# A two-layer hybrid decoder trunk on one core: ScalarE's planned order made to count table loads, and x1 transposed from scaled rows

## The chip, the core and the metric

One core of one Trainium2 chip runs one launch of the kernel. The metric is device time in microseconds (us), the median of the runs of that kernel. Engines are written as in the profile: PE (TensorE; its weight loads are PEld), ACT (ScalarE), DVE (VectorE), POOL (GpSimd), SP (SyncE).

## What is computed

The reference is a trunk of `DEPTH = 2` layers over 512 tokens of width 1024, all in float32. Cut to what matters here:

```python
def hybrid_layer(x, ...):
    h = rms_norm(x, ln_mix_pre)
    # one projection h @ w_in, split into the inputs of three mixers and the gate logits
    y_a = dsa_attention(qa, ka, a_v, iq, ik, i_w)        # A: per query the top 128 keys, softmax over them
    o_b = gated_delta_rule(qb, kb, vb, g, beta)          # B: chunked scan with a triangular inverse
    y_b = rms_norm(o_b, gdn_norm) * silu(b_z)
    o_c = retention(qc, kc, vc)                          # C
    y_c = rms_norm(o_c) * silu(c_g)
    merged = sum(sigmoid(gate_i) * (y_i @ w_branch_i))
    x = x + rms_norm(merged @ w_out, ln_mix_post)        # "x1" below
    ff = square(relu(rms_norm(x, ln_mlp_pre) @ w_up)) @ w_down
    return x + rms_norm(ff, ln_mlp_post)                 # "x2" below
```

## The kernel before

Every large product is made of float32 data split into two parts, hi and lo: `passes` (L1068 to L1071) issues three matmuls for one product, hi by hi, lo by hi and hi by lo. Weights come in slabs of 128 x 1024 (512 KB). For each slab SP issues the load, POOL rounds it to the hi part (`w_hi`, L1046 and L1047), DVE subtracts to get the lo part (`w_lo`, L979, a step called `lo`), and PE uses both. There are two slots, so slab n + 2 is loaded and rounded only after PE is done with slab n. A layer has 136 slabs: 76 in the mixing half, the rest in the MLP.

The mixing half is laid out by a planner, `schedule()`, in plain Python before the kernel is built. It holds a list of steps for PE, ACT and DVE with a cost, their predecessors and a rank (the length of work behind a step). It repeatedly takes the step that can start first; among steps of one engine that could start at the same moment it takes the highest rank. Its result is a fixed order per engine (`PE_ORDER`, `ACT_ORDER`, `DVE_ORDER`), which each engine then follows strictly. Dense products are cut in four pieces (`piece`), so that small products can stand between them. A tail that is written out by hand (the `tail` list: gates and merge of branch B, and `stay` steps) follows the planned part. In it, `every` puts each `lo` step behind the DVE step of a slab.

Steps that the change and the prediction touch:

- ACT's `fin` (L1721 to L1728). It finishes branch C and later branch B, four heads each: `fin_sq` squares (L1719), PE sums over partitions (L1361), `fin` takes Ln (L1726) and Exp (L1728), and DVE multiplies (L2143, L2145). A function that is not in the table set loaded last costs an ACT_TABLE_LOAD, which the build places before it. The code loads the set that has both Ln and Exp before head 0 alone (L1723). The gate steps `cg`, `z`, `gate` and `mgate` use Tanh (L1752, L1758, L1771), for which the other set is loaded. When a Tanh has stood between two heads, Ln and Exp each get a load of their own.
- In the order of before, ACT does, for branch C: `fin 0, gate 2, fin 1, fin_sq 2, fin 2, fin_sq 3, gate 3, fin 3`. The planner counts no table loads.
- The end of the mixing half, on DVE: `merge B 2` first makes four `a_lo` parts (`lo_merged`, L2182), waits for PE's merge slab, and combines (L2197, L2203). Then comes the `lo` step of slab 75, the first slab of the output projection, then `merge B 3` with two more `a_lo` parts.
- The output projection: one slab (k = 0 and 1) for all four token tiles into psM, then the seven "staying" slabs, per token tile t (`out_tile`, L1415). `TURNS` says before which of these seven PE turns a finished x1 tile: `(2, 2): 0` is "while working on token tile 2, before its slab 2, turn x1 tile 0".
- A finished token tile t: ACT squares, DVE multiplies with the gain (L2232), adds (L2248), ACT squares again, DVE makes a 128 x 128 diagonal matrix of the row scales (`diagonal`, L804), PE multiplies x1 by it eight times (`turn_x1`, L1428), which transposes and scales at once. ACT and DVE take hi and lo parts from PSUM (L1807, L2238). The first two MLP slabs are done for tiles 0 to 2 first (`up_tokens`), then tile 3 is turned, then tile 3 is done for both.
- The end: per token tile, DVE makes x2 over 1024 columns (L2344), and SP writes it out (L2354).

## Time and profile before

| | us |
|---|---|
| three runs | 1933.62, 1933.68, 1937.95 |
| median | 1933.68 |
| the profiled execution, as timed | 1936.01 |
| its span in the profile | 1934.2 |
| PE busy in it | 1895.0 (98%) |
| ACT busy, with 29 table loads of 1.28 | 497.0 (26%) |
| DVE busy | 1131.6 (59%) |

The profile lists, for each engine, what it did and what it waited for; a wait is put down to the instruction that came last. "PEclk" in a view of stretches is the granted clock of TensorE: 1.00 is 2.4 GHz, 0.50 is 1.2 GHz. The two layers run the same code one after the other; layer 0 ends and layer 1 begins near 970 us, and the same instruction of layer 1 comes some 957 us after that of layer 0 in the mixing half.

### The profile page before, as it was taken

The page shows a single profiled execution, that of the slowest core. Times are in us where ns is not written, and L with a number is a line of the kernel's source. Part 1 is how long each engine was busy: PE and PEld are TensorE (multiplying, and loading weights), DVE is VectorE, ACT ScalarE, POOL GpSimd, SP SyncE. Part 2 cuts the span into 40 slices and gives each one's busy share as a digit, 9 for nine tenths or more (in the row PEclk, how much of TensorE's full clock was granted, in tenths as well). Part 3 has the DMA queues.
Part 4 walks back from the last instruction along what each step waited for, and adds up shares of the span by engine and source line. Part 5 has one row for each costly group of instructions (what it writes and reads, how often), then busy time and mean ns, then how long its engine had stood idle before and what let it go on. Part 6 is the DMA issues. An engine that isn't in the chain of part 4 may idle for free.

```text
span 1934.2 us, 25057 instructions
## 1 busy us (share of the span) xinstructions
PE 1895.0 (98%) x8862; PEld 1534.1 (79%) x8862; DVE 1131.6 (59%) x1910; ACT 497.0 (26%) x971; POOL 353.9 (18%) x549
## 2 busy tenths in 40 slices
PE   8999999999999999999999999999999999999998
PEld 6877767788788888888878767677888888888886
DVE  6865778843465642454477658887535655425534
ACT  3163352312334100011222533534132331000101
POOL 2221111111220222222112211111102102222220
PEclk9999999999999999999999999999999989999999
DMA  6432222322520422223223322222215222222221
GB/s 240 142 120 82 68 69 80 93 66 66 195 99 20 145 94 94 96 98 98 77 95 102 126 66 77 66 80 87 80 53 217 66 77 97 93 95 96 98 98 55
DMA packets 72478, 186.79 MB, mean 97 GB/s; under 512 B 18304, under 2 KB 30784, under 8 KB 71488
## 3 DMA queue, kind: packets, MB, share of 16 engines
q1 hardware_dynamic: 41328, 152.10, 23.3%
q10 hardware_dynamic: 31056, 33.38, 5.1%
q8 instruction: 66, 1.08, 0.2%
q14 instruction: 28, 0.23, 0.0%
HBM read 174.40 MB, written 11.06 MB: 96 GB/s over the span
## 4 chain that ended last, share of the span: by engine, by line
PE 92%; ACT 4%; DVE 3%; issue 1%; DMA 0%; POOL 0%; SPq 0%; DVEq 0%; ACTq 0%; POOLq 0%
PE psD L1069 23%; PE psD L1071 23%; PE psD L1070 23%; PE psM L1069 4%; PE psM L1070 4%; PE psM L1071 4%; PE psM L1128 2%; PE psM L1142 1%; PE psM L1337 1%; PE psM L1234 1%; PE psM L1135 1%; PE psM L1355 1%; PE psM L1343 1%; PE psM L1361 1%; PE psM L1226 1%
## 5 line engine op out<-in xcount | busy, mean ns | idle before, releaser
L1069 PE MATMUL psD<-a_hi,w_hi 128*128 128x512 f32 (+2 forms) x1488 | 597.7, 402 | 2.4 <-DVE a_lo L2238 1.5
L1071 PE MATMUL psD<-a_hi,w_lo 128*128 128x512 f32 (+2 forms) x1488 | 577.8, 388 | 0.0
L1070 PE MATMUL psD<-a_lo,w_hi 128*128 128x512 f32 (+2 forms) x1488 | 576.8, 388 | 0.0
L979 DVE TENSOR_TENSOR w_lo<-raw,w_hi 128x1024 fp32r<-128x1024 f32 x208 | 254.2, 1222 | 295.9 <-POOL w_hi L1047 294.9
L1046 POOL TENSOR_TENSOR w_hi<-raw,tabs 128x1 fp32r<-128x1 f32 x272 | 65.6, 241 | 1541.7 <-PE psD L1071 1324.0
L1069 PEld LDWEIGHTS psD<-a_hi,w_hi 128*128 128x128 f32 (+1 forms) x1488 | 281.2, 189 | 74.7 <-issue 18.0
L1070 PEld LDWEIGHTS psD<-a_lo,w_hi 128*128 128x128 f32 (+1 forms) x1488 | 281.3, 189 | 58.6 <-issue 4.8
L1071 PEld LDWEIGHTS psD<-a_hi,w_lo 128*128 128x128 f32 (+1 forms) x1488 | 280.9, 189 | 58.4
L1047 POOL TENSOR_SCALAR w_hi<-raw 128x1023 fp32r<-128x1023 f32 x272 | 296.9, 1092 | 0.0
L1836 ACT CAST f_hi<-gt 128x512 f32 x64 | 39.9, 623 | 480.2 <-DVE gt L2270 480.2
L2267 DVE TENSOR_SCALAR gt<-psD 128x512 f32<-128x512 f32 x64 | 44.3, 691 | 140.0 <-PE psD L1071 140.0
L1069 PE MATMUL psM<-w_hi,f_hi 128*128 128x512 f32 x256 | 99.6, 389 | 0.0
L1070 PE MATMUL psM<-w_lo,f_hi 128*128 128x512 f32 x256 | 99.6, 389 | 0.0
L1071 PE MATMUL psM<-w_hi,f_lo 128*128 128x512 f32 x256 | 99.6, 389 | 0.0
L1069 PE MATMUL psD<-y_hi,w_hi 128*128 128x512 f32 x192 | 77.5, 404 | 1.7 <-issue 1.7
L2259 DVE TENSOR_TENSOR w_lo<-raw,w_hi 128x1024 fp32r<-128x1024 f32 x64 | 78.2, 1222 | 1.4 <-POOL w_hi L1047 1.4
L1071 PE MATMUL psD<-y_hi,w_lo 128*128 128x512 f32 x192 | 74.9, 390 | 0.0
L1070 PE MATMUL psD<-y_lo,w_hi 128*128 128x512 f32 x192 | 74.7, 389 | 0.0
L1069 PE MATMUL psD<-w_hi,f_hi 128*128 128x512 f32 x192 | 74.7, 389 | 0.0
L1070 PE MATMUL psD<-w_lo,f_hi 128*128 128x512 f32 x192 | 74.7, 389 | 0.0
L1071 PE MATMUL psD<-w_hi,f_lo 128*128 128x512 f32 x192 | 74.7, 389 | 0.0
L1574 ACT COPY wide<-psD 32x512 f32<-32x512 f32 (+1 forms) x84 | 48.7, 580 | 72.8 <-DVE cqk L1944 21.0
(272 smaller groups left out, 2580.1 us busy)
## 6 DMA issues: line engine op xcount, KB each, us to landing
raw<-in_ws SPq DMA_DIRECT2D x272, 512.0 KB, 3.2
s_raw<-in_wo ACTq DMA_DIRECT2D x14, 512.0 KB, 11.9
out<-x SPq DMA_DIRECT2D x8, 512.0 KB, 5.6
x<-rows_d ACTq DMA_DIRECT2D x4, 1024.0 KB, 5.7
x<-out ACTq DMA_DIRECT2D x2, 2048.0 KB, 8.5
e_raw<-in_wo ACTq DMA_DIRECT2D x8, 512.0 KB, 7.4
tabs<-in_tab SPq DMA_DIRECT2D x1, 2944.0 KB, 12.0
x<-in_x SPq DMA_DIRECT2D x4, 512.0 KB, 5.2
```

The source lines that it names most:

```text
L979: dve.tensor_tensor(w_lo[:, s, :], raw[:, s, :], w_hi[:, s, :].bitcast(F32), ALU.subtract) \
L1046: pool.tensor_tensor(w_hi[:, s, 0:1], raw[:, s, 0:1], T("ones")[:, 0:1], ALU.mult)
L1047: pool.tensor_scalar(w_hi[:, s, 1:], raw[:, s, 1:], 1.0, 1.0, ALU.mult, ALU.mult) \
L1069: pe.matmul(out, lhi, rhi, start=start, stop=False)
L1070: pe.matmul(out, lhi, rlo, start=False, stop=False)
L1071: return pe.matmul(out, llo, rhi, start=False, stop=stop)
L1128: ins = pe.matmul(ps[:, cut(h)], lhs(h), rhs(h), start=True, stop=True)
L1135: ins = pe.matmul(ps[:, h * P // 2:(h + 1) * P // 2], lhs[:, cut(h)], blocks(rhs[:, cut(h)], l, odd), start=True, stop=True)
L1574: sig(act.copy(wt[to:to + n, 6 + r % 2, :], src[at:at + n, :]), "rot_copy" if to + n == P else "rot_part")
L1836: act.copy(f_hi[:, bass.ds(it * 4 + i, 1), :].rearrange("p a s -> p (a s)"), gt[:, i, :]).then_inc(*inc("f_hi", 1, FG // 4))
L2259: dve.tensor_tensor(w_lo[:, s, :], raw[:, s, :], w_hi[:, s, :].bitcast(F32), ALU.subtract) \
L2267: dve.tensor_scalar(gt[:, i, :], psD[i][:, :], 0.0, None, ALU.max) \
```

## The change

Five edits in one:

1. The planner has a table `TABLES` of which steps need which table set. An ACT step that needs another set than the last one is planned 1.28 us longer, and when several ACT steps could start at the same moment, such a step counts with a rank lower by 2.56. The build loads the Ln and Exp set before any `fin` that follows a step of the other set, not before head 0 alone.
2. For x1 tiles 0 to 2, DVE writes scaled rows (two operations of 128 x 512) in place of the diagonal matrix, and PE transposes them against the identity. Tile 3 stays as it was. Tile 2 is turned one slab later.
3. The `a_lo` parts of the merged tiles are DVE steps of their own (`low`), and the `lo` step of slab 75 moves ahead of `merge B 2`.
4. The seven "staying" loads signal on two semaphores (three loads, four loads) in place of seven.
5. In the last layer, x2 is made and written out in halves of 512 columns.

```diff
-TURNS = {(2, 2): 0, (2, 5): 1, (3, 5): 2}
+TURNS = {(2, 2): 0, (2, 5): 1, (3, 6): 2}
...
+TABLES = {"silu": "exp", "cg": "exp", "z": "exp", "gate": "exp", "mgate": "exp", "decays": "log", "fin": "log"}
...
+    def loads(n):
+        return 1.28 if n[0] == "act" and TABLES.get(n[1], tables) != tables else 0.0
...
-            n = max((n for n in names if starts[n] <= first + 1e-9), key=lambda n: rank[n])
+            n = max((n for n in names if starts[n] <= first + 1e-9), key=lambda n: rank[n] - 2 * loads(n))
...
+        t += loads(n)
+        tables = TABLES.get(n[1], tables) if e == "act" else tables
...
+    final = max(s for s in closed if s[1] == "lo")
+    closed.remove(final)
+    for lows, j in (((0, 1, 2, 3), 2), ((4, 5), 3)):
+        i = closed.index(("dve", "merge", "B", j))
+        closed[i:i] = [("dve", "low", k) for k in lows] + ([final] if j == 2 else [])
...
+            def scaled(norm, t):
+
+                r = rstd(norm, t, 1)
+                for half in range(2):
+                    w = slice(half * S, (half + 1) * S)
+                    sig(dve.tensor_scalar(wide[:, t, w], x[:, t, w], r, None, ALU.mult), "rows_" + norm)
...
-                                ins = pe.matmul(x1_T(t, k), x[:, t, cut(k)], wide[:, t, 0:P], start=True, stop=True)
+                                if t < READY:
+                                    ins = pe.transpose(x1_T(t, k), wide[:, t, cut(k)], T("ident"))
+                                else:
+                                    ins = pe.matmul(x1_T(t, k), x[:, t, cut(k)], wide[:, t, 0:P], start=True, stop=True)
...
                     def fin(br, h):
-                        if h == 0:
-                            act.preload_act_table_set("natural_log_exp_and_others")
...
                     def stay(j):
-                        act.wait_ge(*on(f"stay_in{j}", 16))
+                        if j == 0:
+                            act.wait_ge(*on("first_in", 16 * 3))
+                        if j == 3:
+                            act.wait_ge(*on("stay_in", 16 * (len(STAYING) - 3)))
...
+                    tables = "exp"
                     for kind, *args in ACT_ORDER:
+                        if TABLES.get(kind, tables) != tables:
+                            tables = TABLES[kind]
+                            if kind == "fin":
+                                act.preload_act_table_set("natural_log_exp_and_others")
...
-                        diagonal("pre_mlp", t)
+                        if t < READY:
+                            scaled("pre_mlp", t)
+                        else:
+                            diagonal("pre_mlp", t)
...
-                        sig(dve.scalar_tensor_tensor(out=x[:, t, :], in0=wide[:, t, :], scalar=r,
-                                                     in1=x[:, t, :], op0=ALU.mult, op1=ALU.add), "x2")
+                        for w in (slice(0, D),) if layer < DEPTH - 1 else (slice(0, S), slice(S, D)):
+                            sig(dve.scalar_tensor_tensor(out=x[:, t, w], in0=wide[:, t, w], scalar=r,
+                                                         in1=x[:, t, w], op0=ALU.mult, op1=ALU.add), "x2")
```

## Rows read from the trace of the kernel before

**Rows 1.** The page's part 1: busy us, share of the span, instructions.
```profile
PE 1895.0 (98%) x8862; PEld 1534.1 (79%) x8862; DVE 1131.6 (59%) x1910; ACT 497.0 (26%) x971; POOL 353.9 (18%) x549
```

**Rows 2.** Waits of PE over the span: us in total, times, longest.
```profile
PE psM L1361 <- ACT sqs L1719: 5.7, 3, 2.6
PE psM L1069 <- DVE w_lo L979: 2.2, 2, 1.1
PE psM L1142 <- ACT x L1670: 2.2, 2, 1.1
...
PE psM L1343 <- DVE small L2129: 2.0, 2, 1.0
```

**Rows 3.** Groups by line of ACT: table loads in the two lines of `fin`.
```profile
L1726 ACT ACT_TABLE_LOAD x6 | 7.7, 1283 | 0.1
L1728 ACT ACT_TABLE_LOAD x6 | 7.7, 1283 | 0.1
```

**Rows 4.** Stretches: length, PE, PEld, DVE, ACT, POOL busy, PEclk, DMA.
```profile
279.00:281.00 2.00, 2.00 (x7) 1.51 (x6) 1.39 (x4) 1.99 (x3) 0.00 (x0) 0.50 0.00 0
```

**Rows 5.** Stretches, start of layer 1's MLP.
```profile
1584.00:1588.00 4.00, 4.00 (x18) 3.90 (x18) 2.18 (x3) 0.62 (x1) 0.55 (x2) 0.50 0.83 316
```

**Rows 6.** Timeline of DVE (start us, us): MLP ReLU steps 1 and 3, layers 0 and 1.
```profile
624.92 0.69 DVE L2267 TENSOR_SCALAR gt<-psD 128x512 f32<-128x512 f32 x1 [1.18 <-PE psD L1071]
...
633.37 0.69 DVE L2267 TENSOR_SCALAR gt<-psD 128x512 f32<-128x512 f32 x1 [0.90 <-PE psD L1071]
...
1582.28 0.69 DVE L2267 TENSOR_SCALAR gt<-psD 128x512 f32<-128x512 f32 x1 [1.24 <-PE psD L1071]
...
1595.29 0.69 DVE L2267 TENSOR_SCALAR gt<-psD 128x512 f32<-128x512 f32 x1 [4.73 <-PE psD L1071]
```

**Rows 7.** Stretches, the end of the top-k work in layer 0.
```profile
350.00:369.00 19.00, 19.00 (x98) 16.02 (x97) 16.95 (x31) 3.47 (x7) 4.48 (x6) 1.00 0.44 145
```

**Rows 8.** Timeline of PE around the turn of x1 tile 0.
```profile
588.94 0.39 PE L1071 MATMUL psM<-s_hi,a_lo 128*128 128x512 f32 x1
589.16 1.95 PE L1428 MATMUL psM<-wide,x 128*128 128x128 f32 x16
590.87 0.48 PE L1069 MATMUL psM<-s_hi,a_hi 128*128 128x512 f32 x1
```

**Rows 9.** Timeline of PE around eight transposes of attention weights.
```profile
253.48 0.40 PE L1071 MATMUL psD<-a_hi,w_lo 128*128 128x512 f32 x1
253.72 1.03 PE L1142 MATMUL psM<-tabs,pr 128*128 128x128 f32 x8
254.50 0.48 PE L1069 MATMUL psD<-a_hi,w_hi 128*128 128x512 f32 x1
```

**Rows 10.** Groups of DVE by form: a row scale from SBUF over 512 columns.
```profile
L2098 DVE TENSOR_SCALAR sc<-rl,small 128x512 f32<-128x512 f32 x2 | 1.0, 480 | 0.0
```

**Rows 11.** Timeline: DVE's diagonals of x1 tiles 2 and 3, PE's turn of tile 3.
```profile
605.99 0.29 DVE L804 TENSOR_SCALAR wide<-tabs,small 128x128 f32<-128x128 f32 x1
...
617.40 0.29 DVE L804 TENSOR_SCALAR wide<-tabs,small 128x128 f32<-128x128 f32 x1
...
619.32 1.95 PE L1428 MATMUL psM<-wide,x 128*128 128x128 f32 x16
```

**Rows 12.** Timeline at the end of the mixing half: slab 75's rounding, then `merge B 2`.
```profile
556.02 1.51 POOL L1047 TENSOR_SCALAR w_hi<-raw 128x1023 fp32r<-128x1023 f32 x1
...
557.99 1.27 DVE L2197 SCALAR_TENSOR_TENSOR mt<-gt,psD 128x512 f32<-128x512 f32 x2
```

**Rows 13.** Timeline of DVE: the last x2 tile.
```profile
1929.91 1.28 DVE L2344 SCALAR_TENSOR_TENSOR x<-wide,small,x 128x1024 f32<-128x1024 f32 x1
```

**Rows 14.** Stretches at the end of the span.
```profile
1932.50:1933.00 0.50, 0.00 (x0) 0.00 (x0) 0.00 (x0) 0.00 (x0) 0.00 (x0) 0.50 0.99 401
```

**Rows 15.** Timeline of DVE: one round of the top-k search over 512 keys.
```profile
368.76 0.68 DVE L2115 MATCH_REPLACE8 work<-small,work 128x512 f32<-128x512 f32 x1
...
369.47 0.69 DVE L2113 MAX8 small<-work 128x8 f32<-128x512 f32 x1
```

More of the change, by code:

```diff
@@ L388, in schedule @@
     free = {"pe": 0.0, "act": 4.0, "dve": 5.0}
-    end, out = {}, []
+    end, out, tables = {}, [], "log"
+    def loads(n):
+        return 1.28 if n[0] == "act" and TABLES.get(n[1], tables) != tables else 0.0
     dense, halved, acc = [("act", "cv", 3)] * ST, None, None
@@ L804, in diagonal @@
                 sig(dve.tensor_scalar(wide[:, t, 0:P], T("ident"), r, None, ALU.mult), "diag_" + norm)
-            return total, rstd, diagonal
+            def scaled(norm, t):
[3 more added lines that the diff above has]
+                    sig(dve.tensor_scalar(wide[:, t, w], x[:, t, w], r, None, ALU.mult), "rows_" + norm)
+            return total, rstd, diagonal, scaled
         def signals(eng, who):
@@ L1035, in _ @@
                 seen, sig, own = signals(dve, "dve")
-                total, rstd, diagonal = dve_norm(dve, sig, own)
+                total, rstd, diagonal, scaled = dve_norm(dve, sig, own)
                 dve.wait_ge(kept["basics_in"], 16)
@@ L1420, in turn_x1 @@
                     def turn_x1(t):
-                        pe.wait_ge(*on("diag_pre_mlp", t + 1))
                         for i in range(2):
+                            if t < READY:
+                                pe.wait_ge(*on("rows_pre_mlp", 2 * t + i + 1))
+                            else:
+                                pe.wait_ge(*on("diag_pre_mlp", 1))
                             if t == 2:
@@ L1866, in _ @@
                     seen, sig, own = signals(dve, "dve")
-                    total, rstd, diagonal = dve_norm(dve, sig, own)
+                    total, rstd, diagonal, scaled = dve_norm(dve, sig, own)
                     def f32(ap):
@@ L2186, in merge @@
                         b = "AB".index(br)
-                        if b and j >= 2:
-                            for k in (range(4), range(4, 6))[j - 2]:
-                                lo_merged(k)
                         slab(dve, ("merge", br, j))
@@ L2210, in _ @@
                              "split": split_y,
-                             "mergeC": mergeC, "merge": merge, "stay": stay}
+                             "mergeC": mergeC, "merge": merge, "stay": stay, "low": lo_merged}
                     for kind, *args in DVE_ORDER:
@@ L2249, in _ @@
                                                      in1=x[:, t, :], op0=ALU.mult, op1=ALU.add), "x1")
-                        diagonal("pre_mlp", t)
+                        if t < READY:
+                            scaled("pre_mlp", t)
+                        else:
+                            diagonal("pre_mlp", t)
                         for i in {1: (0, 1), 2: (2,)}.get(t, ()):
@@ L2352, in _ @@
                         for t in range(ST):
-                            sp.wait_ge(*on("x2", t + 1))
-                            sp.dma_start(out[:, t * D:(t + 1) * D], x[:, t, :]).then_inc(kept["x_saved"], 16)
-                        sp.wait_ge(kept["x_saved"], 16 * ST * (DEPTH + 1))
+                            for half in range(2):
+                                sp.wait_ge(*on("x2", 2 * t + half + 1))
+                                sp.dma_start(out[:, t * D + half * S:t * D + (half + 1) * S], x[:, t, half * S:(half + 1) * S]) \
+                                    .then_inc(kept["x_saved"], 16)
+                        sp.wait_ge(kept["x_saved"], 16 * ST * (DEPTH + 2))
                 before.update(counted - before)
```

2 lines of the change are left out of this document (1 added, 1 removed).

## The prediction

> **What bounds the kernel now.** I read the page's first part, then the waits of PE, then the stretches around each of those waits, and last the timelines. PE is busy for 1895.0 of 1934.2 us [rows 1], so a change can only pay in three ways: less work on PE, fewer waits of PE, or a shorter head or tail. Outside head and tail the waits are few and all lie in the mixing half and at the x1 tiles. The largest is PE waiting for ACT's squares in `fin`, 5.7 us in three places: 2.6 in each layer and 0.5 in layer 1 [rows 2]. PE waits 1.1 us per layer for the lo part of slab 75, and about 1.0 us each for two steps of the last attention block, per layer [rows 2]. ACT (26%) and DVE (59%) are far from full over the span, but not everywhere: from 350 to 369 us DVE is busy 16.95 of 19.00 us [rows 7]. That stretch is the top-k search, which runs in DVE's fixed order, and work of PE that depends on it can't be moved earlier by a faster PE.
>
> **Table loads.** The groups of ACT show six loads at the Ln and six at the Exp of `fin`, 1283 ns each, with 0.1 us of idle time ahead of them all together [rows 3]. They are the heads 1, 2 and 3 of branch C in two layers. With the load at head 0 and the one at the next gate, branch C has 8 loads per layer, 8 x 1.28 = 10.3 us of ACT in about 20 us. `fin_sq 2` stands behind four of them in ACT's order, and PE waits for it. In the new order I follow the planner's rule. Planned 1.28 us longer, `fin 0` ends late enough that `fin 1` is ready beside `gate 2` and has the higher rank, so the two heads go together under one load. `fin_sq 2` is next by rank, then `gate 2`, `fin_sq 3`, and `fin 2` and `fin 3` together, then `gate 3`. That is four loads in place of eight, and `fin_sq 2` moves ahead of `gate 2`, about 3 x 1.28 = 3.8 us earlier, more than the wait of 2.6. So I take the 5.7 us of wait as gone. What is late next is `gate 2`, some 3 us later; its PSUM bank is wanted again only four dense tiles later, some 20 us. Branch B's four heads stand together already, so nothing changes there. The penalty on the rank acts only when two steps tie, so the planned 1.28 us is what moves things. It moves them from the first `cg` step on, in all three orders, for the rest of the mixing half. I can't cost that from rows; I take zero with both signs kept open in the rivals.
>
> There is a second cost of this wait in the profiled execution. Behind it the granted clock is 0.50 (1.2 GHz), for example from 279 to 281 us [rows 4]; that stretch at half clock costs some 3.4 x 0.5 = 1.7 us. It does not follow the same wait in layer 1. A longer one lies at the start of layer 1's MLP [rows 5]: there the ReLU steps of layer 1 lag those of layer 0 by 1582.28 - 624.92 = 957.36 us before and by 1595.29 - 633.37 = 961.92 us behind it, 4.56 us more [rows 6]. The three timed runs spread over 4.3 us, about one such fall. I leave one of the longer kind in the median of before and after alike.
>
> **x1 as scaled rows.** A turn by the diagonal is 8 matmuls that show as 16 records, and from the last dense matmul before it to the first one behind it 590.87 - 588.94 = 1.93 us pass, less one ordinary step of 0.23: 1.70 us of PE [rows 8]. Eight transposes show as 8 records and take 254.50 - 253.48 = 1.02 less 0.23 = 0.79 us [rows 9]. So each of the three turns saves 0.91 us, 6 x 0.91 = 5.5 us in both layers, all on PE. DVE pays for it: two operations of 128 x 512 with a row scale. The nearest row for one is 0.48 us [rows 10], so 0.96 in place of 0.29. They would be 1.4 if they ran like an ordinary two-operand step (0.69 for each half); I take 0.96, from the row of the same operation. For tile 2 the diagonal was done at 606.28 [rows 11], directly ahead of the turn. Now PE arrives there 2 x 0.91 = 1.8 us earlier, ACT and DVE get tile 2 earlier by the same, and the turn is one slab (6 x 0.23 = 1.4 us) later, which covers the extra 0.67. Behind it only one slab (1.4 us) in place of two (2.7) covers the making of tile 2's hi and lo parts before `up_tokens` wants them, and they can begin only 0.45 earlier after the turn's start, a half turn being that much shorter: little or no slack is left. Tile 3 is similar: its diagonal is done at 617.69 and PE turned it at 619.32 [rows 11], 1.6 us of slack. PE now comes 2.7 us earlier, the chain of tile 3 only 1.2, as ACT's and DVE's hi and lo work on tile 2 stands in its way. Slack about 0.1. I charge 0.25 us per layer for these two near ties.
>
> A rule of the Trainium skill speaks against this edit. In these rows the dense matmul behind the eight transposes starts without a longer step, at the full clock [rows 9]. "TensorE: Matmul & The Clock Gate", Part 4, says of PE's transposes that they do not count as busy time for the monitor that grants the clock. By that rule less counted work at the turns could bring on the fall of the clock that layer 1 shows at its MLP, and the sum would be less favourable by one such fall or two.
>
> **The lo step of slab 75.** Its hi part is rounded by 556.02 + 1.51 = 557.53, and DVE turns to `merge B 2` at 557.99 [rows 12]. So in its new place ahead of `merge B 2` the step doesn't wait for POOL, runs ahead of the four operations of `merge B 2` in place of behind them, and PE's wait goes: 2.2 us in both layers [rows 2], and 0.1 each of a slower first matmul, 2.4. Behind it in DVE's queue stands `merge B 2`, 1.2 us later, and with it two hi parts of ACT. `merge B 3` had waited for the same lo step and those hi parts, so it starts where it did; if it didn't, PE has 24 matmuls of slab 75 (5.5 us) to run before it wants the banks of `merge B 3`. Making the `a_lo` parts steps of their own changes nothing in order. The two semaphores in place of seven: all seven loads have landed when the first `stay` runs (there is no wait of ACT for them), so zero; if they were late, the first copy would wait for two more loads of 1.3 us each.
>
> **Output in halves.** The last x2 runs from 1929.91 for 1.28 us [rows 13]; SP then writes 512 KB, and the transfer runs at up to 401 GB/s [rows 14], so 1.3 us. With halves the second half is written from about 1931.35 (0.15 later) with 0.65 us of transfer left: 0.65 - 0.15 = 0.5, less a second issue, so 0.4. It can't cost more than a second fixed issue, 0.2 us.
>
> **The sum.** 5.7 (waits of `fin`) + 5.5 + 2.4 + 0.4 = 14.0, less 2 x 0.25 = 13.5 us. Part of the 5.7 I expect back as longer waits in the last attention block, where DVE is nearly full [rows 7]: DVE, too, waited in the `fin` block, so most of it moves along; I charge 0.25 per layer. That makes 13.0: 1933.7 - 13.0 = 1920.7 us. Against the profiled execution's own time the half clock behind `fin` goes as well: 1936.0 - 13.0 - 1.7 = 1921.3. That execution lies 2.3 us above the median, and the two agree within 0.6.
>
> **The rivals.**
> - The `fin` part pays nothing (0.22), in one of two ways. Either PE gets to the last attention block earlier and waits there for DVE's top-k in its place; for it speaks the full DVE [rows 7], against it that DVE's own waits in the `fin` block go too. Or the change doesn't do what it says: the planner, whose penalty acts only on ties, still alternates `fin` and gates, the loads stay near eight per layer, and the wait stays. 1920.7 + 5.2 = 1925.9. The count of loads tells the two apart.
> - The new order is better than mine (0.12): with table loads counted, half of the other waits of the attention part, about 2.5 us per layer, goes too. 1920.7 - 5.0 = 1915.7.
> - The clock falls once more, or twice (0.08), at the x1 turns and MLP starts, by the mechanism shown in layer 1 at 4.56 us each [rows 6]: 1920.7 + 4.6 = 1925.3 to 1929.8. The page named above would have this one. For it speaks that the fall in layer 1 came some us after the x1 turns; against it, that layer 0 has the same work and no fall.
> - Slower (0.05): the replanned order puts rounds of the top-k search for the last block behind other work of DVE, and PE, out of dense pieces by then, waits for them. A planner's step of the search is two rounds, 2 x (0.68 + 0.69) = 2.7 us and more [rows 15]. Four such steps late, in two layers, cost 8 x 2.8 = 22.4: 1943.1. It decides from 13.0 + 5.8 = 18.8 us, or 9.4 per layer, between three and four steps late. Against it: in the planner's own reckoning DVE's work doesn't grow, and the rank of these steps is set by hand and unchanged.
>
> **How the numbers follow.** The forecast has 0.53, with its own range from 1917.5 to 1924: the near ties and the unknown replan at 1.5 us per layer each way. The range for 8 in 10 takes in most of the rivals at 1915.7 and 1925.9 and the first fall of the clock: 1914.5 to 1928. A measurement of this kernel can tell 0.3%, 5.8 us, from no change, so faster means below 1927.9: 0.53 + 0.12 + nearly all of 0.22, which has 2 us of margin, and half of 0.08, which makes 0.87; I take 0.85 as falls of the clock differ between runs. Same: 0.10. Slower: 0.05.
>
> **What would show it.** Right: table loads fall from 29 to about 21, none at an Exp; L1361 is gone from PE's waits; `turn_x1` for tiles 0 to 2 shows 48 records where it showed 96, with 0.8 us each on PE; no wait of PE at the first output slab; the last transfer ends some 0.4 us earlier behind PE's end. Wrong: L1361 still waits, or the waits at L1343 and L1142 grow by what it lost; PE waits for x1's rows (L1428's line) or for `a_lo` in `up_tokens` by more than 0.5 us; stretches at PEclk 0.50 behind the turns in both layers. The prediction as a whole fails if the replanned middle of the mixing half, about 170 us per layer, holds waits that before doesn't have.

## The result and the profile after

The changed kernel takes 1921.22 us in the median of 5 runs (1914.49 to 1925.78). The kernel before takes 1933.62 us beside it (5 runs, 1933.08 to 1937.95). The ratio is 0.9926, with a 95% interval of 0.9911 to 0.9942. The forecast was 1920.7 us, faster. The profiled execution of after is the one at 1925.78 us, with a span of 1924.0 us. One run of one experiment, the x1 rows alone, took 2180.43 us at a mean clock of 0.82, a slow execution, and is left out of its times below.

The runs of after spread over 11 us, and they line up with the mean granted clock that each run lists: 1914.49 at 0.999, 1916.91 at 0.998, 1921.22 at 0.996, 1921.44 at 0.995 and 1925.78 at 0.993. So differences of a few us are compared below at equal clock where I can. For the kernel before, the 66 runs beside the experiments give 1931.5 us on average at 0.998 (3 runs), 1933.5 at 0.997 (17), 1934.4 at 0.996 (19), 1935.9 at 0.995 (13), 1937.8 at 0.994 (8) and 1940.8 at 0.993 (5); one run at 0.991 took 1942.5. The clock is listed in steps of 0.001, each about 1.9 us here, so a comparison at equal clock is good to 1 or 2 us, no closer. Where a stretch of the traces holds the whole effect, it is the better measure.

Part 1 of the page of after (busy us, share of the span, instructions) answers [rows 1]:

```profile
PE 1893.1 (98%) x8814; PEld 1533.2 (80%) x8814; DVE 1133.0 (59%) x1920; ACT 486.9 (25%) x963; POOL 352.9 (18%) x549
```

PE has 48 fewer records, ACT has lost 10.1 us. That is eight table loads at 1.28 us, so 21 are left of 29. The waits of PE in after (us in total, times, longest) answer [rows 2]:

```profile
PE psM L1163 <- ACT x L1697: 2.2, 2, 1.1
PE psM L1364 <- DVE small L2162: 2.0, 2, 1.0
...
PE psD L1090 <- DVE a_lo L2267: 1.5, 2, 0.7
```

The two largest removable waits are gone: PE's wait for ACT's squares (`fin`, now L1382) and its wait for the lo part of slab 75. The waits of the attention part are what they were, and no wait has come in their place. Heads 2 and 3 of `fin` in branch C look like this on ACT, layer 0 (start us, us; [rows 3] are its loads before):

```profile
272.99 1.28 ACT L1783 ACT_TABLE_LOAD   x1
...
278.34 1.28 ACT L1814 ACT_TABLE_LOAD   x1
279.63 0.60 ACT L1751 ACTIVATE sqs<-psM 128x512 f32<-128x512 f32 x1
280.26 0.63 ACT L1753 ACTIVATE sqs<-sqs 128x512 f32<-128x512 f32 x1
280.80 0.58 ACT L1751 ACTIVATE sqs<-psM 128x512 f32<-128x512 f32 x1
281.41 0.63 ACT L1753 ACTIVATE sqs<-sqs 128x512 f32<-128x512 f32 x1
282.06 1.28 ACT L1783 ACT_TABLE_LOAD   x1
```

The two heads stand together between one load at L1814 (Ln and Exp) and one at L1783 (Tanh). On PE the sums of heads 2 and 3 now follow each other in one interruption of the dense stream, 4 matmuls together:

```profile
277.00 0.60 PE L1163 MATMUL psM<-tabs,qkv 128*128 128x128 f32 x4
277.44 1.06 PE L1149 MATMUL psM<-qkv 128*128 128x128 f32 x8
278.33 1.88 PE L1382 MATMUL psM<-sqs,tabs 128*128 128x512 f32 x4
279.65 0.79 PE L1090 MATMUL psD<-a_hi,w_hi 128*128 128x512 f32 x1
```

The turn of x1 tile 0, which [rows 8] show before, and the rows of tile 2 on DVE:

```profile
583.72 0.39 PE L1092 MATMUL psM<-s_hi,a_lo 128*128 128x512 f32 x1
583.95 1.03 PE L1453 MATMUL psM<-tabs,wide 128*128 128x128 f32 x8
584.74 0.47 PE L1090 MATMUL psM<-s_hi,a_hi 128*128 128x512 f32 x1
...
599.03 0.88 DVE L825 TENSOR_SCALAR wide<-x,small 128x512 f32<-128x512 f32 x2
```

From the last dense matmul to the next one 1.02 us pass, less the ordinary 0.23: 0.79 us. The list of PE's waits has none for a row. The end of the mixing half, where [rows 12] are those of before:

```profile
552.18 1.51 POOL L1068 TENSOR_SCALAR w_hi<-raw 128x1023 fp32r<-128x1023 f32 x1
554.16 1.21 DVE L1000 TENSOR_TENSOR w_lo<-raw,w_hi 128x1024 fp32r<-128x1024 f32 x1
555.29 1.27 DVE L2226 SCALAR_TENSOR_TENSOR mt<-gt,psD 128x512 f32<-128x512 f32 x2
```

The lo step of slab 75 now stands ahead of `merge B 2`, 0.47 us behind POOL's rounding. Last, the granted clock. In after it falls to 0.50 for some 10 us at the start of the MLP of both layers; before has this only in layer 1 [rows 5]. A shorter fall, of some 3.4 us, lies at 1333 us in after. Stretches (length, PE, PEld, DVE, ACT, POOL busy, PEclk, DMA share, GB/s):

```profile
616.00:620.00 4.00, 4.00 (x24) 4.00 (x23) 2.53 (x3) 0.01 (x1) 1.21 (x2) 0.56 0.67 180
620.00:624.00 4.00, 4.00 (x16) 3.71 (x16) 2.15 (x5) 0.60 (x1) 1.21 (x2) 0.50 0.93 328
...
1576.00:1580.00 4.00, 4.00 (x14) 3.48 (x14) 2.33 (x3) 0.62 (x1) 1.21 (x2) 0.50 1.02 415
```

### The profile page after: what moved, and what is told of

Its sections match the earlier page's. It is cut to its first block, busy times and chain, and to the rows that moved or that the text cites. A ratio compares the mean times of both kernels' runs of the same rounds, so it can differ in the third digit from the quotient of the medians.

```text
span 1924.0 us, 24975 instructions
## 1 busy us (share of the span) xinstructions
PE 1893.1 (98%) x8814; PEld 1533.2 (80%) x8814; DVE 1133.0 (59%) x1920; ACT 486.9 (25%) x963; POOL 352.9 (18%) x549
## 4 chain that ended last, share of the span: by engine, by line
PE 94%; ACT 3%; DVE 2%; issue 1%; DMA 0%; DVEq 0%; SPq 0%; ACTq 0%
PE psD L1090 24%; PE psD L1092 24%; PE psD L1091 24%; PE psM L1092 4%; PE psM L1091 4%; PE psM L1090 4%; PE psM L1149 2%; PE psM L1163 1%; PE psM L1358 1%; PE psM L1255 1%; PE psM L1156 1%; PE psM L1376 1%; PE psM L1364 1%; PE psM L1382 1%; PE psM L1247 1%
```

## The experiments

The first theory is that of the prediction: four separate gains, of which `fin` and the x1 rows carry nearly all. The rivals are that the clock, not the waits, makes a good part of the difference, and that some gains cover or undo each other. I took each part alone on top of before, took one part out of after, and then worked on the two points left over, tile 3's wait and the clock. "Alone" always leaves the rest of before as it is.

### The pair again

Before against itself, and after a second time beside other runs.

> The kernel before, unchanged, to have the granted clock of each of its runs. Theory of the sum: the scatter of 4 to 5 us between runs of one kernel is the number of falls of the clock (some 4.4 us each for a long one, 1.7 for a short one), so a run with fewer falls is faster by that. Run without any: about 1929; most runs at 1933 to 1934 with a mean clock of 0.996 to 0.997; a run at 1938 has a lower mean clock, 0.993 to 0.995. Rival: the scatter is not the clock; runs at 1933 and at 1938 then show the same mean clock.

> The changed kernel, unchanged, for more of its runs with their clocks. Theory of the sum plus falls: without falls (mean clock 0.999) 1914.5 to 1915.5, against 1929.8 for before extrapolated to that clock; each 0.001 of mean clock less costs some 1.5 to 2 us; median 1918 to 1922. If the clock falls as in before, the median is 15 us below before; if rows of x1 bring falls of their own, the median is only 11 to 13 us below, and runs at mean clock 0.996 or less are more than half.

Before again: 1935.14 us, ratio 0.9998 (0.9985 to 1.001); its profile has the waits of [rows 2], only that L1361 has 5.2 us in two places in place of 5.7 in three. The clock is at 0.50 behind the wait of `fin`, this time in both layers (from 278 to 280 us in layer 0). The fall and the missing third wait go together, as is shown below.

After again: 1915.89 us (1913.57 to 1924.62, 6 runs), ratio 0.9912 (0.9892 to 0.9931). That is 5.3 us under the first series of the same kernel. Two of these 6 runs have a mean clock of 0.996 or less, against three of the first 5. Its profile has the clock at full speed where after's first one has it at half:

```profile
616.00:620.00 4.00, 3.98 (x29) 3.58 (x29) 3.00 (x4) 0.62 (x1) 2.37 (x4) 1.00 0.77 226
620.00:624.00 4.00, 4.00 (x19) 3.33 (x18) 3.31 (x5) 0.62 (x1) 0.00 (x0) 1.00 1.01 402
```

At equal clock the two kernels stand apart by 15.0 us at 0.998 (1931.5 against 1916.5, the mean of 1916.91 and 1916.18), 13.3 at 0.996 (1934.4 against 1921.1), 14.4 at 0.995 (one run of after) and 15.6 at 0.993.

### Each part alone

The planner counts loads, the loads are made as needed, and the order follows; nothing else.

```diff
+TABLES = {"silu": "exp", "cg": "exp", ..., "decays": "log", "fin": "log"}
+    def loads(n):
+        return 1.28 if n[0] == "act" and TABLES.get(n[1], tables) != tables else 0.0
-            n = max(..., key=lambda n: rank[n])
+            n = max(..., key=lambda n: rank[n] - 2 * loads(n))
+        t += loads(n)
```

> Edit 1 alone: the planner counts table loads, and the Ln and Exp set is loaded before any fin that follows the other set. Theory of the sum: table loads 21, PE's wait at the fin line gone (5.7 us), no other wait grown by more than 0.5 per layer: 5.2 us less than before at equal clock, so about 1928.5 if the clock falls as often. Rival (given back): the wait appears again at the last attention block (the smax and turn lines), and the time is within 1.5 us of before.

1924.38 us (1922.73 to 1934.41, 7 runs), ratio 0.9947 (0.9929 to 0.9966): 10.4 us under the 1934.8 us of before, twice what was forecast. At equal clock it is 7.0 us (1924.55 against 1931.5 at 0.998) and 6.3 at 0.993 (one run). The wait for the squares is gone, the others are unchanged, and the load order is that of after. Part of it can be read straight off the loads. The stretch from the load at the first gate of branch C to the one at `fin` of branch B is that of these rows, first before again, then this kernel:

```profile
222.07 1.28 ACT L1752 ACT_TABLE_LOAD   x1
...
487.70 1.28 ACT L1723 ACT_TABLE_LOAD   x1
```

```profile
221.91 1.28 ACT L1759 ACT_TABLE_LOAD   x1
...
482.73 1.28 ACT L1793 ACT_TABLE_LOAD   x1
```

265.63 us have become 260.82. In layer 1 it is 265.84 and 261.20. In the profile of before the clock doesn't fall there in layer 1, and the stretch is 264.92 us, so the `fin` part is worth 3.7 to 4.1 us in that layer with no fall of the clock in it. The other traces say the same. Five profiled executions have the order of before, so ten such stretches: 264.46 and 264.92 us without a fall, 265.39 to 265.84 with one fall behind the wait of `fin`, and 266.91 to 267.40 with one there and another some 105 us later. The new order gives 260.49 to 261.50 in 15 stretches without a fall, 260.9 on average; against 264.7, the mean of the two, that is 3.8 us. One fall behind `fin` costs 0.5 to 1.4 us. The rest of the difference of the medians, some 3 us, I put down to the clock, as 6 of 7 runs have a mean clock of 0.998 or 0.999, where most runs of before have 0.995 to 0.997; no trace of those other runs exists.

What the 3.7 to 4.1 us consist of can be read from PE's gaps in layer 1, where neither trace has a fall. First before, then this kernel, with the same small matmuls in the gaps:

```profile
1231.58 0.39 PE L1071 MATMUL psD<-a_hi,w_lo 128*128 128x512 f32 x1
1234.59 1.12 PE L1361 MATMUL psM<-sqs,tabs 128*128 128x512 f32 x2 [2.62 <-ACT sqs L1719]
1235.16 0.79 PE L1069 MATMUL psD<-a_hi,w_hi 128*128 128x512 f32 x1
...
1238.10 0.39 PE L1071 MATMUL psD<-a_hi,w_lo 128*128 128x512 f32 x1
1238.97 1.12 PE L1361 MATMUL psM<-sqs,tabs 128*128 128x512 f32 x2 [0.48 <-ACT sqs L1719]
...
1241.18 0.47 PE L1069 MATMUL psD<-a_hi,w_hi 128*128 128x512 f32 x1
```

```profile
1229.36 0.39 PE L1080 MATMUL psD<-a_hi,w_lo 128*128 128x512 f32 x1
...
1232.24 0.79 PE L1078 MATMUL psD<-a_hi,w_hi 128*128 128x512 f32 x1
```

Before has gaps of 3.58 and 3.08 us from one dense matmul to the next, less 0.23 each: 6.20. The new order has one of 2.88, so 2.65. That makes 3.55 us. The listed waits are 2.62 + 0.48 = 3.10 of it. Another 0.32 comes from how a wait is listed, namely from the end of the record before it: dense matmuls start every 0.23 us, but each record is 0.39 long, so each of these two waits costs 0.16 us more than is listed. For the sums standing in one group only 0.13 is left.

The second wait, of 0.48 us, is there just in the stretches in which the clock doesn't fall behind the first (layer 1 of before, layer 0 of the halves alone, at 281.38 us). With the fall, PE reaches the sums of head 3 later and finds them ready. That is part of why a fall there costs less than the 1.7 us that it takes from PE.

The x1 rows alone. Seven semaphores become two here too, to free some for the new signals of the rows; that edit has no run of its own.

```diff
+                                if t < READY:
+                                    ins = pe.transpose(x1_T(t, k), wide[:, t, cut(k)], T("ident"))
-                        diagonal("pre_mlp", t)
+                        if t < READY:
+                            scaled("pre_mlp", t)
```

> Edit 2 alone, with edit 4 (two semaphores for the staying loads in place of seven, which only frees semaphores). Theory of the sum: each of six turns takes 0.80 in place of 1.70 to 1.77 us on PE, 5.5 in all, less small new waits: the first MLP ReLU step comes 2.6 to 2.8 us earlier behind the end of the mixing half in each layer; about 1928.5 at equal clock. Rival (skill's rule on transposes): the clock falls after the turns in both layers in most runs, mean clock lower than before by 0.002 or more, and the time is 1929 to 1933.

1928.89 us (1928.13 to 1929.77, 6 runs), ratio 0.9963 (0.995 to 0.9976), 5.9 us less. At 0.996 it is 1928.8 against 1934.4, 5.6 less, at 0.995 6.1 less, but at 0.998 (2 runs) only 2.8 less. The trace is clearer. From the last dense matmul ahead of the turn of tile 0 to the first ReLU step of the MLP, 35.98 us pass in before ([rows 8] and [rows 6]); here it is 33.36, in both layers:

```profile
590.80 0.39 PE L1078 MATMUL psM<-s_hi,a_lo 128*128 128x512 f32 x1
...
624.16 0.69 DVE L2286 TENSOR_SCALAR gt<-psD 128x512 f32<-128x512 f32 x1 [1.18 <-PE psD L1078]
```

The eight profiled executions with diagonals have 35.97 to 36.05 there, after again has 33.29 and 33.31. So the rows give 2.6 to 2.7 us per layer, 5.3 in all, on top of before as in after. The wait for the squares stands as it did (5.2 us), so this part adds to the `fin` part. No wait of PE for rows is listed. The recorded rival isn't seen: the mean clock of these runs is 0.995 to 0.998, that of before beside them 0.991 to 0.998, and no MLP in this profile has a fall.

The low steps alone.

```diff
+    final = max(s for s in closed if s[1] == "lo")
+    closed.remove(final)
+    for lows, j in (((0, 1, 2, 3), 2), ((4, 5), 3)):
+        i = closed.index(("dve", "merge", "B", j))
+        closed[i:i] = [("dve", "low", k) for k in lows] + ([final] if j == 2 else [])
```

> Edit 3 alone: the a_lo parts as steps, the lo step of slab 75 ahead of merge B 2. Theory of the sum: PE's wait before the first output slab (1.1 us per layer) goes and nothing comes in its place: 2.4 us less, 1931.2 at equal clock. Rival: merge B 3 becomes later, PE waits for its banks at the first staying slab by about 1 us per layer, and the time is that of before within 0.5 us.

1931.87 us (1929.52 to 1934.22, 12 runs), ratio 0.9978 (0.9967 to 0.9989), 2.9 us less; at 0.997 it is 1931.5 against 1933.5, 2.0 less, and at 0.996 3.2. Here too a stretch is closer. From the load at `fin` of branch B (489.04 us here) to the last dense matmul ahead of the turn of tile 0 (588.90) it is 99.86 us, and 99.87 in layer 1, where before has 588.94 - 487.70 = 101.24 and 101.26. So the step gives 1.4 us per layer, 2.8 in all. The wait of 2.2 us is gone and no new one has come; the largest waits behind the head are these:

```profile
PE psM L1366 <- ACT sqs L1724: 5.2, 2, 2.6
...
PE psM L1147 <- ACT x L1675: 2.2, 2, 1.1
```

The halves of the output alone.

```diff
+                        for w in (slice(0, D),) if layer < DEPTH - 1 else (slice(0, S), slice(S, D)):
+                            for half in range(2):
+                                sp.wait_ge(*on("x2", 2 * t + half + 1))
```

> Edit 5 alone: the last layer's x2 made and written in halves. Theory of the sum: 0.4 us less behind the last matmul; from PE's last instruction to the end of the span 6.7 us in place of 7.1; the median can't tell it. Rival: a second DMA costs more than the overlap gives, the end comes 7.1 us or later behind PE's last.

1932.4 us (1930.42 to 1939.58, 12 runs), ratio 0.9995 (0.9985 to 1.0006): by its time this can't be told from nothing. Its trace tells it. The last matmul of PE in the rows of before, of this kernel and of after:

```profile
1926.70 0.39 PE L1071 MATMUL psD<-w_hi,f_lo 128*128 128x512 f32 x1
```

```profile
1923.32 0.39 PE L1071 MATMUL psD<-w_hi,f_lo 128*128 128x512 f32 x1
```

```profile
1916.92 0.39 PE L1092 MATMUL psD<-w_hi,f_lo 128*128 128x512 f32 x1
```

Their spans are 1934.2, 1930.4 and 1924.0 us. From the end of that matmul to the end of the span 7.11, 6.69 and 6.69 us pass. The spans are given to 0.1 us, but all 14 traces agree: 7.09 to 7.16 with whole tiles (6 traces), 6.64 to 6.71 with halves (8). The halves give 0.4.

### How much of the `fin` part is the loads, how much the order

Here the order of before stays as it is, and only the set that has both Ln and Exp is loaded ahead of each `fin` that needs a load. The planner counts nothing.

```diff
-                        if h == 0:
-                            act.preload_act_table_set("natural_log_exp_and_others")
+                        if TABLES.get(kind, tables) != tables:
+                            tables = TABLES[kind]
+                            if kind == "fin":
+                                act.preload_act_table_set("natural_log_exp_and_others")
```

> The order of before, with the Ln and Exp set loaded before every fin that follows a gate step, but the planner not counting loads. Branch C's order stays fin 0, gate 2, fin 1, fin_sq 2, fin 2, fin_sq 3, gate 3, fin 3. If what pays is the number of loads: ahead of fin_sq 2 stand three loads in place of four, PE's wait at the fin line falls from 2.6 to about 1.3 per layer, 3 us less than before. If what pays is that fin_sq 2 stands ahead of gate 2 in the planner's new order: the wait falls by no more than the one load, and the clock still falls behind it in some runs.

1928.05 us (1926.57 to 1931.96, 7 runs), ratio 0.9965 (0.9953 to 0.9978). 25 loads are left, and part of the wait:

```profile
PE psM L1364 <- ACT sqs L1722: 2.7, 2, 1.4
```

```profile
272.28 0.61 ACT L1759 ACTIVATE wide<-psD 128x512 f32<-128x512 f32 x1
272.91 1.28 ACT L1787 ACT_TABLE_LOAD   x1
...
275.37 0.61 ACT L1722 ACTIVATE sqs<-oc 128x512 f32<-128x512 f32 x1
```

By medians that is 5.8 us less than before, at 0.998 3.4, where the expectation had 3. The Tanh of `gate 2` (at 272.28) still has a load on either side ahead of the squares of head 2. One load fewer stands before them than before, and PE's wait is shorter by about one load: 2.6 to 1.35 us per layer. The stretch between the two loads named above is 262.59 and 262.45 us. So making one load of two gives about 2.4 us of the 3.7 to 4.1 per layer, and the new order gives the rest, some 1.5. The clock stayed high in this kernel too (0.998 or 0.999 in 6 of 7 runs), though PE still waits 1.4 us there.

### After with the x1 part undone

The diagonals for all tiles come back, with `turn_x1(2)` at its old place; everything else is that of after. It ran in two series.

```diff
-TURNS = {(2, 2): 0, (2, 5): 1, (3, 6): 2}
+TURNS = {(2, 2): 0, (2, 5): 1, (3, 5): 2}
-                        if t < READY:
-                            scaled("pre_mlp", t)
-                        else:
-                            diagonal("pre_mlp", t)
+                        diagonal("pre_mlp", t)
```

> The changed kernel with edit 2 undone: x1 tiles 0 to 2 are turned by the diagonal matrices again, tile 2 at its old place. Theory of the sum: 5.0 to 5.5 us more than the changed kernel at equal clock, so about 1920 without falls and 1924 to 1926 in the median. Rival (the transposes bring on the falls): mean clock 0.998 to 0.999 in most runs, above that of the changed kernel, and the median within 2.5 us of the changed kernel's.

> The changed kernel with edit 2 undone, a second time, for more runs with their clocks. If transposes bring on falls: at most one run at 0.996 or less, as the first time (1 in 6), while the kernels with rows in this series show 4 in 10 or more. If it is chance or place in time: both kinds show the same share.

1920.24 us (1919.78 to 1925.64, 6 runs), ratio 0.9929 (0.9913 to 0.9944), and 1920.52 us (1919.67 to 1925.08, 6 runs), ratio 0.9928 (0.9914 to 0.9943). At a mean clock of 0.999 they average 1920.2 us (8 runs), and after averages 1914.4 us (4 runs): 5.8 less, where the forecast had 5.5 and the stretches give 5.3. But only 2 of these 12 runs have a clock of 0.996 or less. In the series of after 5 of 11 have. So in the medians the difference between the kernels shrinks: 1920.2 and 1920.5 against 1921.2 in after's first series and 1915.9 in its second. The x1 part may bring on the fall that costs it its gain in some runs. The next runs go after that.

### The place of the turn of tile 2

`turn_x1(2)` goes back to where before has it, one slab earlier.

```diff
-TURNS = {(2, 2): 0, (2, 5): 1, (3, 6): 2}
+TURNS = {(2, 2): 0, (2, 5): 1, (3, 5): 2}
```

> The changed kernel with tile 2 turned at its old place, one slab earlier. The rows of tile 2 are then done about 0.5 to 0.6 us after PE arrives (before: the diagonal was ready 0.1 us ahead, rows take 0.6 us longer, PE and the tile's chain both come 1.8 earlier). Theory of the sum: PE waits at that turn, 0.3 to 0.8 us per layer, and nothing is gained behind it, as tile 3's chain sets the next point: up to 1 us more than the changed kernel at equal clock. Rival: no wait, the move was not needed; equal time, and tile 2's lo parts come earlier.

1917.05 us (1913.70 to 1920.23, 4 runs), ratio 0.990 (0.988 to 0.992); at 0.999 it is 1913.8 against 1914.4. PE's list has no wait for the rows, but the turn itself shows one: from the last dense matmul to the next one it takes 1.24 us here, 1.02 in after (start and length of the two, in this kernel):

```profile
598.68 0.39 PE L1092 MATMUL psD<-s_hi,a_lo 128*128 128x512 f32 x1
...
599.92 0.48 PE L1090 MATMUL psD<-s_hi,a_hi 128*128 128x512 f32 x1
```

The rows are made from 598.53 to 599.41 us, and PE begins on them at 599.08. Layer 1 has 1.25. The wait at tile 3 is 0.73 us where after has 0.72, first here, then after:

```profile
613.80 0.33 PE L1090 MATMUL psD<-a_hi,w_hi 128*128 128x128 f32 x1 [0.73 <-DVE a_lo L2267]
```

```profile
614.15 0.33 PE L1090 MATMUL psD<-a_hi,w_hi 128*128 128x128 f32 x1 [0.72 <-DVE a_lo L2267]
```

To the first ReLU step this kernel has 33.50 and 33.60 us, against 33.29 to 33.36. So the new place covers 0.2 us per layer, less than the 0.3 to 0.8 expected, and the medians can't tell it. Two of the 4 runs have a clock of 0.996 or less, and the profiled one has the long fall in layer 1's MLP, so the new place isn't needed for it.

### The wait at tile 3

PE stops 0.7 us per layer behind `turn_x1(3)`, for `a_lo` of tile 3, in before and after alike. Here the last k of the second MLP slab for tiles 0 to 2 is held back and put behind that turn, as cover. In a second kernel tile 3 comes from scaled rows as well.

```diff
+HELD = 1
-                            up_tokens(i, 0, READY)
+                            up_tokens(i, 0, READY, range(KT - HELD) if i else range(KT))
+                                up_tokens(1, 0, READY, range(KT - HELD, KT))
```

> The changed kernel, with the last eighth of the second MLP slab for tiles 0 to 2 (three matmuls of 384 columns, 0.5 us) moved behind the turn of tile 3, where PE waits 0.72 us for tile 3's lo parts. Theory of the sum: the wait shrinks to 0.2 to 0.4, 0.3 to 0.4 us per layer gained. Rival on falls: if the clock falls at the start of the MLP because of that wait, long falls there become rarer: at most 1 run in 6 at a mean clock of 0.996 or less, against 5 in 11 of the changed kernel.

> As the one with the held eighth, and tile 3 is turned from scaled rows too. Theory of the sum: the turn takes 0.9 us less of PE, but its rows are ready 0.6 us later than the diagonal; hi and lo parts start 0.2 to 0.5 us earlier; 1.0 to 1.3 us in both layers below the changed kernel at equal clock, 1913 without falls. Rival on falls (transposes bring them on): more long falls, more than half of the runs at a mean clock of 0.996 or less, and the median above that of the changed kernel.

With the held k: 1915.36 us (1913.16 to 1916.86, 5 runs), ratio 0.9898 (0.9883 to 0.9913). The wait falls to 0.4 us in both layers together:

```profile
PE psD L1091 <- DVE a_lo L2269: 0.4, 2, 0.2
```

With tile 3 from rows too: 1914.58 us (1913.96 to 1914.91, 5 runs), ratio 0.9892 (0.9878 to 0.9907). The turn is shorter by 0.9 us, but PE then stands earlier at what is made behind it, and some 0.6 of the 0.9 goes into waits:

```profile
PE psD L1091 <- DVE a_lo L2269: 1.3, 2, 0.7
...
PE psM L1454 <- DVE wide L826: 0.3, 2, 0.2
```

To the first ReLU step the first has 33.07 us in both layers and the second 32.71, against 33.29 to 33.36 in after, rows alone and after again where the clock holds. So the held k gives 0.2 to 0.3 us per layer and both together 0.6, close to what was expected (0.3 to 0.4, and 0.5 to 0.65). In the times this is at the edge of what can be told: at 0.999 (one run each) 1913.2 and 1914.6 against 1914.4 of after, at 0.998 (four runs each) 1915.9 and 1914.5 against 1916.5 (two runs). The spread is narrower: all ten runs have a clock of 0.998 or 0.999, and they lie between 1913.2 and 1916.9. The last one has the lowest median of this study, 20.5 us below its own before, or 1.1%.

Mean clocks of 0.996 or less, over the kernels that have lost the wait of `fin`, in whole or in part:

| kernels | runs | of them at 0.996 or less |
|---|---|---|
| diagonals, tile 3's wait as before (tables alone, preload alone, after with diagonals twice) | 26 | 4 |
| rows for tiles 0 to 2, tile 3's wait as before (after twice, turn in its old place) | 15 | 7 |
| rows, with the held k | 10 | 0 |

The tables alone ran on another chip than the later series; without them the first row is 3 of 19. The expectation had 4 in 10 or more for the kernels with rows in the last series and found 2 of 14, both with the turn in its old place. By chance alone a difference like 7 of 15 against 4 of 26 comes about once in 16 times (Fisher's exact test), one like 7 of 15 against 0 of 10 once in 50.

A mean clock doesn't say where the clock fell. The 14 profiled executions do, read in stretches of 1 us from 8 us on to 6 us before the end. In them a fall comes in two sizes: a short one takes about 1.7 us of full clock (3.4 us at 0.50), a long one about 5.1 (10.2 us at 0.50). They begin at these times (us):

| kernel | short | long |
|---|---|---|
| before | 278 | 1582 |
| before again | 277, 974, 1237 | |
| rows alone | 277, 383, 1233 | |
| low steps alone | 277, 382, 973, 1236, 1342 | |
| halves alone | 1234, 1340 | |
| tables alone; preload alone; after again | | |
| after | 1333 | 616, 1572 |
| after with diagonals, twice | 966; 967 | |
| after, turn in its old place | 965 | 1566 |
| held k; held k and all rows | 964; 965 | |

All long falls stand at the start of an MLP: 3 in the 8 MLPs with rows and tile 3's wait (rows alone, after twice, turn in its old place), 1 in the 16 with diagonals, none in the 4 with the held k.

The falls right behind `fin` (277 and 278, 1233 to 1237) are only in the executions with its full wait, 8 in their 10 layers; none of the nine that have lost it, in whole or in part, has one there. So the change takes these falls away with the wait, and half of the wait was enough for it (preload alone). So a mean clock of 0.996 need not be a long fall: the low steps alone have 0.995 from five short ones.

## Why the prediction was right, point by point

- **The time.** Forecast 1920.7, measured 1921.2 in the series it is held against. That is closer than the reasoning earned, and in part luck: the second series has 1915.9. At equal clock the change is worth 13.3 to 15.6 us where the sum had 13.0. The traces give 3.7 to 4.1 us per layer for `fin`, 5.3 for the rows, 2.8 for the lo step and 0.4 for the halves, some 16 us. Against that stood the clock: the forecast left one long fall "in the median of before and after alike", and the profiled execution of after has two.
- **The `fin` wait.** The step was right, the term too small. It was 5.7 less 0.5 given back, so 5.2 for both layers; it measures 3.7 to 4.1 per layer, that is 7.4 to 8.2 in the stretches, and 6.3 to 7.0 in the runs at equal mean clock. The wait is gone, as forecast, and nothing was given back: the waits of the last attention block are the same to 0.1 us. So the term was too small by 1 to 3 us. It counted the listed idle time alone, in an execution in which the fall in layer 0 hides the second wait of 0.48 us. Without falls the waits are 3.1 us in each layer, PE's gaps shrink by 3.55, and 0.2 to 0.6 more lies outside these gaps and stays open.
- **The order.** 21 loads, four in place of eight in branch C, as forecast. My hand-followed order was wrong in one detail: `fin_sq 2` doesn't move ahead of `gate 2`. The order that runs is `fin 0, fin 1, gate 2, fin_sq 2, gate 3, fin_sq 3, fin 2, fin 3`. The wait goes because two loads stand ahead of `fin_sq 2` where four stood (the one ahead of head 0 counted in both), and because PE's `fin 2` is placed later. That is argued from the order lists and the rows of ACT at 272.99 and 278.34; the run with the old order and fewer loads (wait 1.35 us in place of 2.6) is what shows that each load ahead of the squares counts.
- **x1 rows.** Forecast 0.91 us per turn and 5.5 in all, less 0.5 for two near ties; the turn takes 0.79 where it took 1.70, and the stretches give 5.3. The two row operations take 0.88 against 0.96. So the near ties cost about 0.1 per layer and not 0.25: the wait at tile 3 is 0.7 per layer as before, and for rows none is listed. Of tile 2's new place I said that it covers the extra DVE time; the run with the old place shows 0.2 us per layer that it covers.
- **The lo step.** Forecast 2.4, measured 2.8 in the stretches (2.9 by medians). From the last matmul on the slab before to the first on slab 75, before has 561.87 - 560.36 = 1.51 us, less 0.23: 1.28, where the list says 1.12, and the next matmul is late by 0.1. The term took the listed wait, which is 0.16 us short of what is lost, in each layer. `merge B 3` starts in the trace at 559.89 against 563.72, and the rounding by POOL ends at 553.69 against 557.53: 3.83 and 3.84 us earlier, so against that rounding it starts where it did, as I said.
- **The halves.** Forecast 0.4, measured 0.4. The 0.2 us that I set for a second issue as the most it could cost had no row.
- **The clean pair.** Tables alone and after again have profiled executions with no fall in the table above. Their spans are 1920.9 and 1912.0 us, 8.9 apart. For what lies between them (rows, lo step, halves) the forecast had 5.5 - 0.5 + 2.4 + 0.4 = 7.8, and the stretches have 5.3 + 2.8 + 0.4 = 8.5.
- **The half clock behind `fin`.** I valued it at 1.7 us. The stretches give 0.5 to 1.4. PE's second wait, of 0.48 us, goes when the clock falls, so part of what the fall takes had been idle time; the rest of the difference is not traced.
- **The rival that the clock falls once more (0.08).** This one came true in part, in the profiled execution itself. The ReLU step answers [rows 6]. In after, layer 0:

```profile
617.44 0.69 DVE L2299 TENSOR_SCALAR gt<-psD 128x512 f32<-128x512 f32 x1 [1.54 <-PE psD L1092]
...
630.12 0.69 DVE L2299 TENSOR_SCALAR gt<-psD 128x512 f32<-128x512 f32 x1 [4.42 <-PE psD L1092]
```

Between the two 12.68 us pass, where before has 633.37 - 624.92 = 8.45 [rows 6]: 4.23 us for this fall, against the 4.56 that I had for one. (The first of the two steps is late as well: it comes 33.72 us behind the dense matmul ahead of the turns, against 33.35 in layer 1, so 0.37 more.) Layer 1 has a second one, 1585.51 - 1572.50 = 13.01, so 4.56. The forecast had 1925.3 for one such fall and 1929.8 for two, and the profiled execution took 1925.78 with two long ones. In the second series two runs of six have a mean clock of 0.996 or less; whether they had long falls no trace shows. Its chance of 0.08 looks too low, though its size was right. The rule in the Trainium skill, "TensorE: Matmul & The Clock Gate", Part 4, that PE's transposes don't count as busy for the clock, is what named it. The counts lean to it (7 of 15 with rows against 4 of 26 with diagonals; 3 of 8 MLPs against 1 of 16 in the traces), and the kernels with the held k lean away: all rows, more transposes, and no run of 10 with a low mean clock. The rows alone lean away too, with no long fall in their profile. In the rows the dense matmul right behind a turn by transposes runs at full speed (0.47 us at 584.74), but that says little of a fall that begins some 15 us behind the last of these turns (601.56 against 616.5). Nor are transposes needed: before has its long fall with diagonals. They may bring a fall more often together with the 0.7 us in which PE waits at tile 3, right ahead of the stretch that falls; no run shows that.

What stays open: no run tells the transposes from the time at which PE arrives at the MLP, and the counts could still be the draw. A kernel with diagonals and the held k wasn't run. The share of the time of a median that is due to falls is argued from the listed clocks, not shown run by run, as only one run of each series has a trace.

## What to carry to other kernels

When ACT stands ahead of PE, count its table loads in the order, and load the set that holds all functions of the next step; here two functions of one set cost two loads for each head because each found its own. Price a wait by the whole interruption of the dense stream around it, from one dense matmul to the next, not by the listed idle time: each of the three waits looked at here cost 0.16 us more than listed, and a fall of the clock in the profiled execution hid another wait of 0.48. So 2.6 us of wait seen in layer 0 were worth 3.7 to 4.1. And once differences reach 0.3%, list the clock beside each run and compare runs at equal clock; look at where the clock fell, too. The kernels that cover the 0.7 us of wait ahead of the MLP had steadier times here (10 runs), though it isn't shown that the covering is why.

## What the runs showed of the chip that I had not expected

- **The price of a fall depends on its place.** Behind `fin` 3.4 us at a clock of 0.50 cost 0.5 to 1.4 us, at the start of the MLP 10.2 us at 0.50 cost 4.2 to 4.6. The engine had been through an idle 0.7 us before the latter, then a run of matmuls over 128 columns; in after's layer 0 the wait ends at 614.15, and the stretch from 616 is the one that falls. The same wait and the same matmuls stand in after again, in both layers, with no fall.
- **A kernel's mean clock tells its time.** Over 66 runs of before, 0.993 to 0.998 goes with 1940.8 to 1931.5 us, about 1.9 us for each 0.001. The rows alone don't follow it so closely (1928.7 at 0.998, 1928.8 at 0.996).
- **A wait of PE costs more than its listed time.** Dense matmuls start every 0.23 us and each record lasts 0.39, so the idle time behind the last one starts 0.16 us late: 2.62 listed for 2.78 lost, 0.48 for 0.64, 1.12 for 1.28.
- **A table load costs what its record shows.** The Trainium skill, "ScalarE: Activation LUTs", section "What ACT_TABLE_LOAD costs", has a drain of about 1380 ns beside the 1283 ns of the load. The traces here don't show it: the Ln behind the load at 278.34 starts at 279.63, 0.01 us behind its end, and the load itself starts 0.03 us behind the end of the squares at 277.69 + 0.62 = 278.31. By that page's 2.66 us the eight loads removed would be 21 us of ACT; ACT's busy time shrank by 10.1.
